# Packing the time-step columns into four partition groups, moving the parameter loads to SyncE's queue, and starting two output blocks behind the scan

## The chip, the cores and the metric

The kernel runs on one core of one Trainium2 chip. The metric is the device time in microseconds of one execution (us). TensorE (PE) does the matmuls, and its weight loads are listed as PEld; VectorE (DVE), ScalarE (ACT) and GpSimd (POOL) do the elementwise work; SyncE (SP) and the other engines issue transfers (a DMA issue of ScalarE's own queue is listed as ACTq, of SyncE's as SPq).

## The reference, cut to what matters

The whole is a decoder step with two layers over 512 prompt tokens and 64 sample tokens (8 sequences of 8), 576 tokens in all, model width 1024. Layer 0 is a Mamba-2 mixer (2048 inner channels, 32 heads) and an MLP, layer 1 a sparse attention and an MLP. The change touches layer 0's mixer alone:

```
zxbcdt = h @ in_w                                  # 1024 -> z 2048, x/B/C 3072, dt 32
z, xbc, dt = split(zxbcdt)
xbc, new_conv = causal_conv(xbc, conv_state, conv_w, conv_b)      # 4 taps, then silu
dt = softplus(dt + dt_bias)                        # one number for each token and head
A = -exp(a_log)                                    # the scan uses x*dt and a = dt*A
y, h_last = ssd_scan(xs * dt, dt * A, B, C, h0)    # chunks of 128 tokens
y = (y + xs * d_skip) * silu(z)
y = y * rsqrt(mean over each of 4 groups of y*y + eps) * norm_w
mix = y @ out_w                                    # 2048 -> 1024
h = layer_norm(alpha * h + mix)
```

## The kernel before

**Layout.** Activations lie feature by partition: `xT` holds the input as 8 chunks of 128 features by 576 tokens. Every dense product is done in fp32r with both operands split into a rounded part (hi) and the rest (lo), and three products (hi·hi, hi·lo, lo·hi) are summed. A weight slot is 128 x 1024 numbers (512 KB). There are two slots: SyncE loads one into `ring` (L596 for the first two, L603 for the others), ScalarE writes its hi part (`split_hi`, L943, semaphore `w_hi`), GpSimd its lo part (`split_lo`, L697, semaphore `w_split`), then the ring slot may be loaded again. A block is one slot times all tokens: `dense_block` (L1299) runs over 8 chunks k, three products, two halves of 288 tokens, so 48 matmuls, into one of two pairs of PSUM banks; `w_used` tells that a block is done, `blk_evac` that its banks have been read.

**Start.** ScalarE first issues the loads of `dtw` (the 32 time-step columns of the weights, L930), of x in four parts of 2 chunks (L932, 576 KB each) and of 12 parameter tiles (L934, 0.72 MB together: bias and log A in `dtb`, identity, triangles, masks, conv weights, norms). Then it splits slot 0, rounds x into `xs[:, 0]` (L983, chunk by chunk), and splits slot 1. VectorE makes the lo part of x (L1822, semaphore `x_split`). TensorE first does the time-step product with `dtw` in plain fp32: for each k a matmul of 512 prompt tokens into bank `bX` and one of 64 sample tokens into `bM`, both into partitions 0 to 31 (L1360, L1361). In the trace each fp32 matmul is two instructions. Then come blocks 0 to 9 of group 0.

**Time steps.** ScalarE waits for all parameters (`s_par`) and for the product, adds the bias, takes the absolute value and exp (L989 to L993) on 32 x 576. VectorE computes softplus with a polynomial (L1825 to L1837: 17 operations on 32 x 576, one of them a reciprocal, most of them waiting for the one before) and only then turns to the causal conv of blocks 0 to 4 (L1851 for 512 tokens and L1853 for 64, three of each for a block). After block 4 TensorE transposes the steps and a = dt·A to token by head (L1371, L1372, 10 transposes), and VectorE copies them out (`dt_tok`, `a_tok`), which lets `segment_rows` and the decays start.

**ScalarE's order in blocks 0 to 9** is written out by hand:

```
for blk in range(GB):
    evac(blk)
    split_hi(blk + 2)
    if blk:
        conv_silu(blk - 1)
```

`evac` copies the block's banks to `raw` (L1011 to L1014) and writes the first conv tap (L1021 to L1024). `conv_silu(blk - 1)` (L1040) waits until VectorE has finished that block's conv. Whatever stands behind it in this order waits too.

**Scan.** 20 tiles (4 groups g, 5 token tiles c) follow; between the parts of a tile TensorE does "filler" blocks: the next group's input blocks, or in the last group the first half of the output projection. The last group's y is squared and summed over partitions (`squares_sum`, L1491), VectorE and ScalarE form the root and its reciprocal (L1884, L1059, L1889), scale y (L1891), round it (L1064) and make its lo part (L1974, semaphore `y_split`). Then comes `last_projection(0, ...)`: the second half of the output projection, 8 blocks that sum over y's tiles 8 to 15. Tiles 8 to 11 are of group 2 and are ready earlier, 12 to 15 are of the last group. Its block 0 waits chunk by chunk for `y_split`, the means of the layer norm (L1336) follow block 1. `finish_his` and `finish_los` split the later slots.

Of the kernel before, what the change touches and what calls it, by code (L numbers as in the profile page):

```python
# [28 lines left out]
ACT = mybir.ActivationFunctionType  # L29
AX = mybir.AxisListType  # L30

P = 128
D = 1024
KC = D // P
NP_TOK = 512
NB, NS = 8, 8
ND = NB * NS
T = NP_TOK + ND
HT = T // 2
# [6 lines left out]
MH, MP, MN, MG = 32, 64, 128, 4  # L46
# [23 lines left out]
NSLOT = 2  # L70
NT = 5
# [14 lines left out]
def build(nc, a):  # L86

    with ExitStack() as ctx:
# [8 lines left out]
        dense = ctx.enter_context(nc.psum_tensor("dense", [P, 4, 512], F32))  # L97
# [3 lines left out]
        bX, bM = bXM[:, 0, :], bXM[:, 1, :]  # L101
# [4 lines left out]
        split = sb("split", [P, NSLOT, 2, SLOT], F32R)  # L106
        ident = sb("ident", [P, P])
        triu = sb("triu", [P, 2, P])
# [19 lines left out]
        def carve(*shape, parts=P):  # L128

            first = at[0]  # L130
            at[0] += int(np.prod(shape))
            assert at[0] <= ARENA, at[0]
            tiles.append(nc.alloc_sbuf_tensor_at(f"tile{len(tiles)}", [parts, *shape], F32,
                                                 offset=arena_at + 4 * first, align_bytes=4))
            return tiles[-1][tuple(slice(0, n) for n in (parts, *shape))]
# [6 lines left out]
        xT = carve(KC, T)  # L142
# [15 lines left out]
        y_lo = split_tile("y_lo", at[0] - DI // P * T, DI // P, T)  # L158
        y_hi = xs.rearrange("p s k t -> p (s k) t")
        at[0] = xs_end  # L160
        dtT = carve(T, parts=MH)
        dw = [carve(T, parts=MH) for _ in range(4)]
        aT = carve(T, parts=MH)
        at[0] = xs_end + (XB + DI // P) * T
        cst = carve(NXB, NB, 3)
        lastp = carve(NXB, 3)
# [3 lines left out]
        nw = carve(DI // P)  # L170
        dsk = carve(DI // P)
        dtw = carve(KC, MH)
        dtb = carve(2, parts=MH)
        smask = carve(NB, parts=ND)
        dt_tok = carve(NT, MH)
        a_tok = carve(NT, MH)
# [110 lines left out]
        S_M1, S_M2, s0 = [], [], SL_IN + SL_OUT  # L287
        B_OUT = (SL_IN, SL_IN + KC)
        B_M1, B_M2, b0 = [], [], SL_IN + 2 * KC
        for layer in range(2):  # L290
# [6 lines left out]
            if layer == 0:  # L297
# [3 lines left out]
                s0, b0 = S_O + SL_O, B_O + KC  # L301
        assert s0 == N_SLOTS

        PARAM_TILES = ((dtw, "dtw"), (dtb, "dtb"), (ident[:, :], "ident"), (triu[:, :, :], "triu"),
                       (low[:, :, :], "low"), (smask, "smask"), (cst, "cst"), (cw, "cw"), (cb, "cb"),
                       (nw, "nw"), (dsk, "dsk"), (lng[:, :, :], "lng"), (lnb[:, :, :], "lnb"))
        N_PARAMS = len(PARAM_TILES)
# [8 lines left out]
        s_par = sem("params_loaded")  # L316
# [3 lines left out]
        w_split = sem("slots_split")  # L320
        w_used = sem("slots_used")
# [8 lines left out]
        blk_evac = sem("block_evacuated")  # L330
# [8 lines left out]
        dt_tok_ready = sem("dt_by_token")  # L339
# [118 lines left out]
        def link(eng, who, ins):  # L458

            s = dve_step if who == "dve" else act_step  # L460
            ins.then_inc(s, 1)
            steps[who] += 1
            eng.wait_ge(s, steps[who])

        def width(c):
            return P if c < 4 else ND

        def tok(c):
            return slice(c * P, c * P + width(c))
# [124 lines left out]
        def _(sp):  # L594
# [3 lines left out]
            def stream(first, last):  # L598
                with sp.Fori(first // NSLOT, last // NSLOT) as i:
                    for j in range(NSLOT):  # L600

                        sp.wait_ge(w_split, i * NSLOT + (j + 1 - NSLOT))
                        sp.dma_start(ring[:, j, :], a["w"][i * NSLOT + j, :, :]).then_inc(w_ready[j], 16)  # L603

            stream(NSLOT, S_OUT[0] + 2 * NSLOT)

            sp.wait_ge(xbc_ready, NXB)
# [320 lines left out]
        def _(act):  # L928
            for dst, name in PARAM_TILES[:1]:
                act.dma_start(dst, a[name]).then_inc(s_dtw, 16)  # L930
            for q in range(4):
                act.dma_start(xT[:, 2 * q:2 * q + 2, :], a["x"][:, 2 * q:2 * q + 2, :]).then_inc(s_x[q], 16)  # L932
            for dst, name in PARAM_TILES[1:]:
                act.dma_start(dst, a[name]).then_inc(s_par, 16)  # L934

            def split_hi(s, i=None):

# [48 lines left out]

            act.wait_ge(s_par, 16 * (N_PARAMS - 1))
            act.wait_ge(dt_done, 1)
            act.activation(dtT[:, 0:NP_TOK], bX[0:MH, :], ACT.Identity, bias=dtb[:, 0:1])  # L989
            link(act, "act", act.activation(dtT[:, NP_TOK:T], bM[0:MH, 0:ND], ACT.Identity, bias=dtb[:, 0:1]))  # L990
            link(act, "act", act.activation(dw[0], dtT, ACT.Abs))
            act.activation(dw[1], dw[0], ACT.Exp, scale=-1.0)
            act.activation(dtb[:, 1:2], dtb[:, 1:2], ACT.Exp).then_inc(dt_abs, 1)  # L993
# [72 lines left out]
            for g, c, n in TILES:  # L1066
                L = width(c)
# [94 lines left out]
            for own in range(2):  # L1162
                for m in range(4):
                    kv, gp = divmod(m, 2)
                    for half in range(2):
                        ps = slice(half * HD, half * HD + HD)
                        src = kvT[ps, m, 0:NP_TOK].rearrange("p (c j h) -> p j h c", c=NCMP, h=2)
# [106 lines left out]
        def _(pe):  # L1274
# [43 lines left out]
            def by_token(out, part, v):  # L1318
# [3 lines left out]
                                   start=True, stop=True)  # L1322
                return mm

            def last_projection(k, hi, lo, ready=None):

                b0, s0, nsl, _ = ENDS[k]
                for j in range(2):
                    dense_block(b0 + j, s0 + j * nsl, nsl, hi, lo, ready=ready if j == 0 else None)

                pe.wait_ge(blk_evac, b0 + 1)
                if k == 0:

                    pe.wait_ge(st_ready, MG * (4 + NB))
                for cols in (slice(0, 512), slice(512, T)):
                    mm = pe.matmul(flat_x[:, cols], onesd[:, :], xT[:, 0, cols], start=True, stop=True)  # L1336
                mm.then_inc(ln_tok, 1)
                with pe.Fori(1, KC // 2 - 1) as i:
                    for j in range(2):
                        dense_block(b0 + j, s0 + j * nsl, nsl, hi, lo, i, 2 * nsl)  # L1340
                dense_block(b0 + KC - 2, s0 + (KC - 2) * nsl, nsl, hi, lo)

                def squares(kk):
                    if kk == nsl * KC - 2:
                        pe.wait_ge(ln_added, 6 * (k + 1))
                        by_token(s2, 0, SQS[k])

                dense_block(b0 + KC - 1, s0 + (KC - 1) * nsl, nsl, hi, lo, after=squares)
# [8 lines left out]
            for k in range(KC):  # L1357
                pe.wait_ge(s_x[k // 2], 16)
                ends = dict(start=k == 0, stop=k == KC - 1)
                pe.matmul(bX[0:MH, :], dtw[:, k, :], xT[:, k, 0:NP_TOK], **ends)  # L1360
                mm = pe.matmul(bM[0:MH, 0:ND], dtw[:, k, :], xT[:, k, NP_TOK:T], **ends)  # L1361
            mm.then_inc(dt_done, 1)
            in_block(0, (x_split, 0))
            for blk in range(1, 5):
# [1 line left out]
            pe.wait_ge(s_par, 16 * (N_PARAMS - 1))  # L1366

            pe.wait_ge(dt_ready, 1)
            for c in range(NT):
                L = width(c)  # L1370
                pe.transpose(bX[0:L, c * 64:c * 64 + MH], dtT[:, tok(c)], ident[0:MH, 0:MH])  # L1371
                mm = pe.transpose(bX[0:L, c * 64 + MH:c * 64 + 64], aT[:, tok(c)], ident[0:MH, 0:MH])  # L1372
            mm.then_inc(dt_tr, 1)
            in_block(5)
            in_block(6)
# [2 lines left out]
            for c in range(NT):  # L1378
                L = width(c)
                pe.matmul(bS[0:L, 0, c * MH:(c + 1) * MH], low[0:L, c // 4, 0:L], a_tok[0:L, c, :],  # L1380
                          start=True, stop=True)
            for c in range(4):
                pe.matmul(bS[:, 0, (NT + c) * MH:(NT + c + 1) * MH], ones[:, :], a_tok[:, c, :],
                          start=True, stop=True)
            pe.matmul(bS[:, 1, 0:NB * MH], ones[0:ND, :], am.rearrange("p b h -> p (b h)"),
                      start=True, stop=True).then_inc(dec_sum, 1)
# [429 lines left out]
        def _(dve):  # L1816
# [51 lines left out]
                conv(blk)  # L1868

            dve.wait_ge(dt_tr, 1)  # L1870
            tr = bX[:, 0:NT * 64].rearrange("p (c k h) -> p c k h", c=NT, k=2)
            dve.tensor_copy(dt_tok[:, 0:4, :], tr[:, 0:4, 0, :])
            dve.tensor_copy(dt_tok[0:ND, 4, :], tr[0:ND, 4, 0, :])
            dve.tensor_copy(a_tok[:, 0:4, :], tr[:, 0:4, 1, :])
            dve.tensor_copy(a_tok[0:ND, 4, :], tr[0:ND, 4, 1, :]).then_inc(dt_tok_ready, 1)
            for blk in range(5, GB):
                conv(blk)

# [570 lines left out]
```

## Time and profile before

| what | value |
|---|---|
| time before, median of 3 runs | 2104.06 us (2100.3 to 2104.97) |
| profiled execution: its time | 2098.91 us |
| profiled execution: span | 2097.2 us |
| TensorE busy | 1942.2 us (93%) |
| VectorE, ScalarE, GpSimd busy | 816.4, 705.8, 961.4 us |
| granted clock of TensorE, mean | 0.952 |

The span runs from the first instruction to the last; times in views are counted from its start. The granted clock is the share of TensorE's 2.4 GHz that it was given (1.00, or 0.50 for 1.2 GHz; a value between them is a stretch with both). An idle time in square brackets is that of the instruction's own engine before it, with the releaser behind the arrow.

### The profile page before, as it was taken

The page shows a single profiled execution, that of the slowest core. Times are in us where ns is not written, and L with a number is a line of the kernel's source. Part 1 is how long each engine was busy: PE and PEld are TensorE (multiplying, and loading weights), DVE is VectorE, ACT ScalarE, POOL GpSimd, SP SyncE. Part 2 cuts the span into 40 slices and gives each one's busy share as a digit, 9 for nine tenths or more (in the row PEclk, how much of TensorE's full clock was granted, in tenths as well). Part 3 has the DMA queues.
Part 4 walks back from the last instruction along what each step waited for, and adds up shares of the span by engine and source line. Part 5 has one row for each costly group of instructions (what it writes and reads, how often), then busy time and mean ns, then how long its engine had stood idle before and what let it go on. Part 6 is the DMA issues. An engine that isn't in the chain of part 4 may idle for free. (4 is left out here: it accounts for less than half of the span.)

```text
span 2097.2 us, 36461 instructions
## 1 busy us (share of the span) xinstructions
PE 1942.2 (93%) x14668; PEld 1773.5 (85%) x14668; DVE 816.4 (39%) x1567; ACT 705.8 (34%) x1292; POOL 961.4 (46%) x685
## 2 busy tenths in 40 slices
PE   7998899988888998999999999899978899999996
PEld 5987887867778998999998998755548899999996
DVE  7364573746455220022233112378655521012134
ACT  4453553634134221122223131266533322122222
POOL 2445454444447643356444342454403565346552
PEclk9998999989998999999999999799999899999998
DMA  4211312113131226332221333420161122222221
GB/s 163 80 51 41 121 51 111 51 70 127 41 117 62 80 72 172 90 121 82 81 79 51 127 136 109 173 78 1 41 222 41 51 81 90 81 81 80 82 82 64
DMA packets 61077, 185.12 MB, mean 88 GB/s; under 512 B 15519, under 2 KB 20287, under 8 KB 59425
## 3 DMA queue, kind: packets, MB, share of 16 engines
q1 hardware_dynamic: 48720, 130.18, 18.9%
q0 software_dynamic: 9952, 50.08, 6.7%
q10 hardware_dynamic: 2288, 3.23, 0.4%
q8 instruction: 83, 1.36, 0.3%
q14 instruction: 34, 0.27, 0.0%
HBM read 167.05 MB, written 27.35 MB: 93 GB/s over the span
## 5 line engine op out<-in xcount | busy, mean ns | idle before, releaser
L1299 PE MATMUL dense<-xs,split 128*128 128x288 f32 x6848 | 978.3, 301 | 28.2 <-POOL xs L805 8.5
L1299 PEld LDWEIGHTS dense<-xs,split 128*128 128x128 f32 x6848 | 942.0, 192 | 63.2 <-issue 43.5
L697 POOL TENSOR_TENSOR split<-ring,split 128x1024 fp32r<-128x1024 f32 x212 | 533.7, 2518 | 815.7 <-ACT split L943 793.7
L943 ACT ACTIVATE split<-ring 128x1024 fp32r<-128x1024 f32 x212 | 223.9, 1056 | 798.2 <-PE dense L1299 775.4
L1299 PE MATMUL dense<-hid,split 128*128 128x288 f32 x3072 | 415.8, 298 | 5.8 <-POOL split L697 5.8
L1299 PEld LDWEIGHTS dense<-hid,split 128*128 128x128 f32 x3072 | 414.3, 191 | 6.0 <-POOL split L697 6.0
L1863 DVE SCALAR_TENSOR_TENSOR tile<-tile,dense 128x576 f32<-128x576 f32 (+1 forms) x56 | 42.2, 754 | 422.0 <-PE dense L1299 422.0
L2032 DVE TENSOR_SCALAR sq<-dense 128x576 f32<-128x576 f32 x64 | 48.5, 757 | 310.5 <-PE dense L1299 310.5
L914 POOL TENSOR_SCALAR tile<-tile,tile,tile 128x128 f32<-128x128 f32 (+3 forms) x128 | 77.8, 622 | 80.8 <-DVE tile L2195 80.8
L1851 DVE SCALAR_TENSOR_TENSOR tile<-tile,tile,tile 128x512 f32<-128x512 f32 x72 | 87.5, 1215 | 41.2 <-ACT tile L1024 39.4
L816 POOL TENSOR_TENSOR hid<-sq,hid 128x576 f32 x64 | 77.3, 1208 | 0.0
L1201 ACT ACTIVATE tile<-tile,tile 128x128 f32<-128x128 f32 (+3 forms) x128 | 70.4, 553 | 18.1 <-DVE tile L2180 17.9
L1632 PE MATMUL dense<-tile,tile 128*128 128x128 f32 x576 | 66.4, 274 | 0.8 <-issue 0.8
L1632 PEld LDWEIGHTS dense<-tile,tile 128*128 128x128 f32 x576 | 64.9, 188 | 1.9 <-issue 1.2
L1998 DVE SCALAR_TENSOR_TENSOR tile<-tile,tile 128x576 f32<-128x576 f32 x24 | 61.8, 2575 | 0.0
L1148 ACT ACTIVATE hid<-sq 128x576 f32 x64 | 43.9, 686 | 44.3 <-DVE sq L2035 44.3
L1299 PE MATMUL dense<-y_lo,split 128*128 128x288 f32 x256 | 56.6, 303 | 0.0
L1672 PE MATMUL dense<-tile,tile 64*128 64x128 f32 (+3 forms) x128 | 47.8, 491 | 6.1 <-DVE tile L2172 4.6
L1715 PE MATMUL dense<-tile,tile 128*64 128x256 f32 x384 | 52.0, 392 | 0.0
L1672 PE MATMUL bS<-tile,tile 64*128 64x128 f32 (+3 forms) x128 | 49.1, 496 | 0.4 <-DVE tile L2135 0.4
L2035 DVE TENSOR_TENSOR sq<-sq 128x576 f32<-128x576 f32 x64 | 48.6, 759 | 2.2
L1028 ACT ACTIVATE tile<-dense 128x576 f32<-128x576 f32 x16 | 10.4, 652 | 108.3 <-PE dense L1299 108.3
(316 smaller groups left out, 2118.2 us busy)
## 6 DMA issues: line engine op xcount, KB each, us to landing
ring<-in_w SPq DMA_DIRECT2D x212, 512.0 KB, 3.3
tile<-in_state POOLq DMA_DIRECT2D x4, 2048.0 KB, 9.2
o_sssm<-tile POOLq DMA_DIRECT2D x4, 2048.0 KB, 7.5
tile<-in_cmp POOLq DMA_DIRECT2D x32, 256.0 KB, 3.2
tile<-in_win POOLq DMA_DIRECT2D x8, 1024.0 KB, 5.9
tile<-in_sel SPq DMA_DIRECT2D x32, 256.0 KB, 5.2
o_kv<-tile POOLq DMA_DIRECT2D x1, 3456.0 KB, 12.2
bskew<-bscr SPq DMA_DIRECT2D x1, 3072.0 KB, 22.3
```

The source lines that it names most:

```text
L697: pool.tensor_tensor(split[:, j, 1, :], ring[:, j, :], split[:, j, 0, :].bitcast(F32), ALU.subtract).then_inc(w_split, 1)
L816: pool.tensor_tensor(hid[:, 1, m, :], sq[:, j, :], hid[:, 0, m, :].bitcast(F32), ALU.subtract).then_inc(hid_ready, 1)
L914: last = pool.tensor_scalar(pb(u, r)[:, 0:n], pb(u, r)[:, 0:n], wt[:, u % 2, r:r + 1], gate, ALU.mult, ALU.mult)
L943: act.activation(split[:, j, 0, :], ring[:, j, :], ACT.Copy).then_inc(w_hi, 1)
L1201: last = act.activation(pb(u, r)[:, 0:n], pb(u, r)[:, 0:n], ACT.Exp, bias=nmx[:, u % 4, r:r + 1], accum_out=sm[:, u % 4, r:r + 1])
L1299: mm = pe.matmul(dense[:, 2 * par + h_, 0:HT], split[:, j, w, cols], v[:, kk, h_ * HT:(h_ + 1) * HT], start=kk == 0 and t == 0, stop=kk == ...
L1632: mm = pe.matmul(dense[:, 2 * (s_ % 2) + kv, r * P:(r + 1) * P], cw1[:, kv, r, j, :], rows, start=j == 0, stop=j == 7)
L1672: pe.matmul(SB[k][:, 0:(qt + 1) * P], qT[half_of(h_), gp * GR + r, tok(qt)], kvT[half_of(h_), 4 * (br + 1) + gp, 0:(qt + 1) * P], start=Tr ...
L1715: mm = pe.matmul(OBANK[half_of(g), rr * 2 * P:(rr + 1) * 2 * P], v, PT[t % 4][:, h_ * 2 * P:(h_ + 1) * 2 * P], start=br == 0 and kt == 0, ...
L1851: dve.scalar_tensor_tensor(o[:, 0:NP_TOK], r[:, k:k + NP_TOK], cw[:, x, k:k + 1], o[:, 0:NP_TOK], ALU.mult, ALU.add)
L1998: link(dve, "dve", dve.scalar_tensor_tensor(xT[:, m, :], xT[:, m, :], alpha, CEN[k], ALU.mult, ALU.subtract))
L2035: dve.tensor_tensor(h, h, h, ALU.mult).then_inc(hid_sq, 1)
```

## The change

1. The time-step product gives four prompt tiles of 128 tokens in partitions 32q to 32q+31 (q = 0 to 3) of `bX`, 128 columns wide, and the 64 sample tokens four times over in `bM`. So `dtT`, `dw` and `aT` become 128 partitions x 192 columns; `dtb` is loaded four times. The softplus works on 128 x 192, and 4 transposes (two of 128 x 128) take the place of 10.
2. SyncE issues the parameter loads (now 15) behind the first two slots and ahead of the rest of the weights; ScalarE issues only `dtw` and x.
3. In the last projection of layer 0, blocks 0 and 1 are done as chunks 0 to 3 of both, then chunks 4 to 7 of both.

```diff
-        dtT = carve(T, parts=MH)
-        dw = [carve(T, parts=MH) for _ in range(4)]
-        aT = carve(T, parts=MH)
+        dtT = carve(P + ND)
+        dw = [carve(P + ND) for _ in range(4)]
+        aT = carve(P + ND)
...
-        dtb = carve(2, parts=MH)
+        dtb = carve(2)
...
-        PARAM_TILES = ((dtw, "dtw"), (dtb, "dtb"), (ident[:, :], "ident"), (triu[:, :, :], "triu"),
+        PARAM_TILES = ((dtw, "dtw"), *((dtb[q * MH:(q + 1) * MH], "dtb") for q in range(4)), (ident[:, :], "ident"), (triu[:, :, :], "triu"),
...
+            for dst, name in PARAM_TILES[1:]:
+                sp.dma_start(dst, a[name]).then_inc(s_par, 16)
             stream(NSLOT, S_OUT[0] + 2 * NSLOT)
...
-            for dst, name in PARAM_TILES[1:]:
-                act.dma_start(dst, a[name]).then_inc(s_par, 16)
...
-            act.activation(dtT[:, 0:NP_TOK], bX[0:MH, :], ACT.Identity, bias=dtb[:, 0:1])
-            link(act, "act", act.activation(dtT[:, NP_TOK:T], bM[0:MH, 0:ND], ACT.Identity, bias=dtb[:, 0:1]))
+            act.activation(dtT[:, 0:P], bX[:, 0:P], ACT.Identity, bias=dtb[:, 0:1])
+            link(act, "act", act.activation(dtT[:, P:P + ND], bM[:, 0:ND], ACT.Identity, bias=dtb[:, 0:1]))
...
+            def early_chunks(b0, s0, hi, lo, ready):
+                for ks in (range(0, 4), range(4, KC)):
+                    for j in range(2):
+                        if ks[0] == 0:
+                            pe.wait_ge(blk_evac, b0 + j - 1)
+                            pe.wait_ge(w_split, s0 + j + 1)
+                        for k in ks:
+                            if j == 0:
+                                pe.wait_ge(ready[0], ready[1] + k + 1)
+                            for t, (w, v) in enumerate(((0, hi), (0, lo), (1, hi))):
+                                for h_ in range(2):
+                                    mm = pe.matmul(dense[:, 2 * ((b0 + j) % 2) + h_, 0:HT],
+                                                   split[:, (s0 + j) % NSLOT, w, k * P:(k + 1) * P],
+                                                   v[:, k, h_ * HT:(h_ + 1) * HT],
+                                                   start=k == 0 and t == 0, stop=k == KC - 1 and t == 2)
+                        if ks[0]:
+                            mm.then_inc(w_used, 1)
...
+                if k == 0:
+                    early_chunks(b0, s0, hi, lo, ready)
                 for j in range(2):
-                    dense_block(b0 + j, s0 + j * nsl, nsl, hi, lo, ready=ready if j == 0 else None)
+                    if k:
+                        dense_block(b0 + j, s0 + j * nsl, nsl, hi, lo, ready=ready if j == 0 else None)
...
-                pe.matmul(bX[0:MH, :], dtw[:, k, :], xT[:, k, 0:NP_TOK], **ends)
-                mm = pe.matmul(bM[0:MH, 0:ND], dtw[:, k, :], xT[:, k, NP_TOK:T], **ends)
+                for bank, n in ((bX, P), (bM, ND)):
+                    for q in range(4):
+                        mm = pe.matmul(bank[q * MH:(q + 1) * MH, 0:n], dtw[:, k, :],
+                                       xT[:, k, q * P:q * P + n] if n == P else xT[:, k, NP_TOK:T], **ends)
...
-            for c in range(NT):
-                L = width(c)
-                pe.transpose(bX[0:L, c * 64:c * 64 + MH], dtT[:, tok(c)], ident[0:MH, 0:MH])
-                mm = pe.transpose(bX[0:L, c * 64 + MH:c * 64 + 64], aT[:, tok(c)], ident[0:MH, 0:MH])
+            for i, src in enumerate((dtT, aT)):
+                o = i * NT * MH
+                pe.transpose(bX[:, o:o + P], src[:, 0:P], ident[:, :])
+                mm = pe.transpose(bX[0:ND, o + P:o + NT * MH], src[0:MH, P:P + ND], ident[0:MH, 0:MH])
...
-            tr = bX[:, 0:NT * 64].rearrange("p (c k h) -> p c k h", c=NT, k=2)
-            dve.tensor_copy(dt_tok[:, 0:4, :], tr[:, 0:4, 0, :])
+            tr = bX[:, 0:NT * 64].rearrange("p (k c h) -> p k c h", k=2, c=NT)
+            dve.tensor_copy(dt_tok[:, 0:4, :], tr[:, 0, 0:4, :])
```

## Rows read from the trace of the kernel before

**Rows 1.** Waits of TensorE, 0 to 60 us (total us, times, longest).

```profile
PE bXM L1360 <- DMA tile<-in_x: 7.7, 1, 7.7
PE dense L1299 <- POOL split L697: 6.9, 1, 6.9
```

**Rows 2.** Timeline, 0 to 60 us (start us, length us, engine, line).

```profile
9.78 1.28 ACT L943 ACT_TABLE_LOAD   x1 [9.78 <-issue]
...
12.04 4.68 ACT L983 ACTIVATE xs<-tile 128x576 fp32r<-128x576 f32 x8
...
12.74 9.34 DVE L1822 TENSOR_TENSOR xs<-tile,xs 128x576 fp32r<-128x576 f32 x8 [12.74 <-ACT xs L983]
...
18.28 26.21 PE L1299 MATMUL dense<-xs,split 128*128 128x288 f32 x192
...
22.48 3.74 DVE L1826 RECIPROCAL tile<-tile 32x576 f32<-32x576 f32 x1
...
27.03 0.75 DVE L1828 TENSOR_TENSOR tile<-tile 32x576 f32<-32x576 f32 x1
...
28.30 9.60 DVE L1831 SCALAR_TENSOR_TENSOR tile<-tile,tile 32x576 f32<-32x576 f32 x7
28.36 2.95 POOL L697 TENSOR_TENSOR split<-ring,split 128x1024 fp32r<-128x1024 f32 x1 [5.86 <-ACT split L943]
...
41.13 0.91 DVE L1866 MEMSET tile<- 64x1024 f32 x1 [0.27 <-issue]
...
42.73 0.28 DVE L1853 SCALAR_TENSOR_TENSOR tile<-tile,tile,tile 128x64 f32<-128x64 f32 x1
...
45.01 0.69 ACT L1040 ACTIVATE tile<-tile 128x576 f32<-128x576 f32 x1 [9.10 <-DVE tile L1853]
...
48.88 2.34 POOL L697 TENSOR_TENSOR split<-ring,split 128x1024 fp32r<-128x1024 f32 x1 [11.59 <-ACT split L943]
...
51.37 7.94 PE L1299 MATMUL dense<-xs,split 128*128 128x288 f32 x48 [6.88 <-POOL split L697]
```

**Rows 3.** DMA issues by line: first and last start, then time to landing.

```profile
L596 SPq DMA_DIRECT2D ring<-in_w x2: 387/404/422, 0.9 to 1.3; - x2
DMA to landing us min/median/max: 4.0/4.9/5.9
L932 ACTq DMA_DIRECT2D tile<-in_x x4: 451/495/723, 1.3 to 3.1; - x4
DMA to landing us min/median/max: 6.2/7.5/8.6
L934 ACTq DMA_DIRECT2D lnb<-in_lnb x1: 504/504/504, 9.2 to 9.2; - x1
DMA to landing us min/median/max: 5.9/7.3/8.2
```

**Rows 4.** The time-step product by line (ns min/median/max, first and last start).

```profile
L1360 PE MATMUL bXM<-tile,tile x16: 592/592/1061, 7.7 to 17.6; 128*32 128x512 f32 x16
```

**Rows 5.** Timeline of TensorE, fp32 matmuls onto 32 partitions each.

```profile
556.05 1.92 PE L1432 MATMUL bXM<-tile,tile 128*32 128x512 f32 x16
...
1533.88 1.70 PE L1782 MATMUL dense<-tile,tile 128*32 128x64 f32 x88 [1.10 <-ACT tile L1252]
```

**Rows 6.** Timeline behind the scan, 587 to 610 us.

```profile
596.00 2.76 DVE L1974 TENSOR_TENSOR y_lo<-tile,xs 128x576 fp32r<-128x576 f32 x4
...
596.81 0.85 PE L1299 MATMUL dense<-xs,split 128*128 128x288 f32 x2 [5.96 <-DVE y_lo L1974]
...
608.07 1.19 PE L1336 MATMUL bXM<-tile,onesd 128*128 128x512 f32 x4
```

**Rows 7.** Idle TensorE in the scan (timeline).

```profile
136.12 1.09 PE L1406 MATMUL bXM<-ident,tile 128*128 128x128 f32 x4 [2.22 <-DVE tile L1957]
```

**Rows 8.** Windows: length, busy of PE, PEld, DVE, ACT, POOL, clock, DMA share, GB/s.

```profile
136.10:139.00 2.90, 2.88 (x14) 2.90 (x15) 1.09 (x3) 2.88 (x4) 1.76 (x1) 0.50 0.02 6
...
596.80:600.00 3.20, 3.19 (x13) 3.19 (x14) 1.96 (x3) 0.09 (x1) 0.00 (x0) 0.50 0.00 0
```

More of the change, by code:

```diff
@@ L1870, in _ @@
             dve.wait_ge(dt_tr, 1)
-            tr = bX[:, 0:NT * 64].rearrange("p (c k h) -> p c k h", c=NT, k=2)
-            dve.tensor_copy(dt_tok[:, 0:4, :], tr[:, 0:4, 0, :])
-            dve.tensor_copy(dt_tok[0:ND, 4, :], tr[0:ND, 4, 0, :])
-            dve.tensor_copy(a_tok[:, 0:4, :], tr[:, 0:4, 1, :])
-            dve.tensor_copy(a_tok[0:ND, 4, :], tr[0:ND, 4, 1, :]).then_inc(dt_tok_ready, 1)
+            tr = bX[:, 0:NT * 64].rearrange("p (k c h) -> p k c h", k=2, c=NT)
+            dve.tensor_copy(dt_tok[:, 0:4, :], tr[:, 0, 0:4, :])
+            dve.tensor_copy(dt_tok[0:ND, 4, :], tr[0:ND, 0, 4, :])
+            dve.tensor_copy(a_tok[:, 0:4, :], tr[:, 1, 0:4, :])
+            dve.tensor_copy(a_tok[0:ND, 4, :], tr[0:ND, 1, 4, :]).then_inc(dt_tok_ready, 1)
             for blk in range(5, GB):
```

## The prediction

> **What bounds the kernel now.** I read the page first: TensorE is busy for 93% of the span, so a change counts only where TensorE stands idle or works longer than it must. The list of TensorE's waits in the first 60 us [rows 1] has two entries: 7.7 us until the first part of x has landed, and 6.9 us at block 4, which has no split weights yet. The timeline of that stretch [rows 2] tells why. Blocks 0 to 3 run without a gap from 18.28 to 44.49 us, 6.55 us each. The next one starts at 51.37, released by GpSimd's lo part, which itself sat idle for 11.59 us for ScalarE's hi part. ScalarE had been idle for 9.10 us in the silu of block 0's conv, released by VectorE's last conv operation at 45.0. VectorE could not begin a conv before 42: it was at the softplus polynomial from 22 to 41 us. So the wait of 6.9 us is VectorE's softplus, handed on through ScalarE's order and GpSimd. The second place is behind the scan [rows 6]: TensorE has done chunks 0 to 3 of the output block and is idle for 5.96 us until VectorE's first `y_split` of the last group. Both waits are longer than they look, because TensorE comes back at its lower rate: block 4 takes 7.94 us in place of 6.55 [rows 2], and from 596.8 to 600 the granted clock is 0.50, which is 1.2 GHz [rows 8].
>
> **Part 1a, the softplus on 128 x 192.** A VectorE operation with two tensors takes 0.75 us at 576 columns and 0.28 at 64 [rows 2], so 0.28 + 128/512 x 0.47 = 0.40 at 192 and 0.43 with the step to the next. The number of partitions should not matter: the 128-partition conv row lies on the line of the 32-partition one only if it doesn't, and I have no other row. Eleven operations of this kind make 4.7 us, the reciprocal a third of 3.74 = 1.25, five with one tensor at most 0.3 each = 1.5. Sum 7.4. In the kernel before, the 17 take 19 us, of which some 4 us are two operations held while GpSimd runs a lo part: the seven of the polynomial take 9.60 where 7 x 0.78 = 5.5 would do, with a GpSimd operation of 2.95 us inside [rows 2]. One such hold may fall into the shorter chain: 7.4 to 9.8, I take 8.6. ScalarE's four operations ahead of it get shorter too, which I count at nothing.
>
> **Part 1b, the time-step product.** The number of columns is 4 x 128 for the prompt as before, but 4 x 64 in place of 64 for the samples, and there are 16 instructions for each k in place of 4. What decides is whether products onto different groups of 32 partitions overlap. They do in the scan [rows 5]: 16 fp32 instructions of 512 columns take 1.92 us where one alone lasts 0.43 behind another (592 ns with its fixed part, [rows 4]), so nearly four at a time. 88 of 64 columns take 1.70 us, 0.019 each. Then a k costs 8 x 128/512 x 0.12 = 0.24 plus 8 x 0.019 = 0.15, together 0.39 at the full rate and 0.7 to 0.8 at half of it. Before, a k took 1.9 us at first (1061 ns an instruction) and 1.0 later (592 ns), in all 10.6 us from 7.7 to 18.28 [rows 2, 4]. Eight k are now at most 6 us, so the arrival of x bounds this stage. If they don't overlap, a k is 1.28 at the full rate: (512 + 256)/(512 + 64) times 0.97. The Trainium skill, TensorEngine Tiling (Array Packing), section "Instruction Overhead", speaks against thin tiles: each matmul has about 60 cycles of overhead, and one should not tile a dimension that is small already. By it, and calling this an estimate, the 128 instructions are not under 3.2 us at 2.4 GHz (6.4 at 1.2), against 3.1 (about 6) by the rows; the sum would be the same by either.
>
> **Part 2, the parameters on SyncE.** ScalarE issued 12 loads at about 0.5 us each up to 9.75, and only then could load its table and split slot 0 (9.78, ready at 12.04), although slot 0 had landed at 0.9 + 4.0 = 4.9 us [rows 2, 3]. Now it is ready for slot 0 at 4.9, so slot 0 is split by 8.5, and x's chunks are rounded as they land (0.6 us each, VectorE's lo part 0.76 each without a hold). On SyncE 15 issues take 1.75 to 9.4 us. Nothing behind them is late: the next slot was issued at about 14.7, behind the lo part of slot 0, and now can go at 9.4. But transfers share the 16 DMA engines. Before, the parameters stood behind x in one queue, and x's parts landed at 7.5 to 11.7 us. How two queues share is to be seen at slot 1: it landed at 1.3 + 5.9 = 7.2, together with x's first part at 7.5, so about half each. Between those two x rows 3 x 0.59 MB pass in 4.2 us, 0.42 MB/us. With equal shares, 0.72 MB of parameters and 0.5 MB of the next slot get ahead of x: 1.22/0.42 = 2.9 us, x complete at 14.6. Unshared, it is 11.7. The Trainium skill, DMA: Bandwidth & Descriptors, section "Queues, rings and completion order", says that each DMA engine takes its queue rows in turn, packet by packet. The two landings agree; by it x lands at 14.6, without it the sum below would be 2.9 us more of a gain. I take 14.6.
>
> Last two k of the product after 14.6: 1.4 us at half rate, so block 0 begins at 16.0. Its chunks are never late: the last x chunk is rounded at 15.8 and its lo part is there by 17. The work ahead of it now has gaps, so the clock may still be at 1.2 GHz for the first 3 us; I charge 0.7 (between 0 and 1.5). Block 0 ends at 16.0 + 6.55 + 0.7 = 23.2, against 18.28 + 6.55 = 24.8. **Gain 1.6** (1.0 to 2.4; 3.9 to 5.3 with x unshared).
>
> Then the chain behind it: ScalarE splits slot 1 (to 16.9; its lo part by 19.4, before block 1), waits for the parameters (the last issued at 9.0 lands 5.9 to 8.2 us later [rows 3], so by about 16) and hands over at 18.3. VectorE is done at 27, with the memset of 0.9 at 28, and needs 3.0 us for a conv (5.4 with a hold): block 0's is done by 31 to 33.5. ScalarE wants it for the silu once block 1's evacuation and slot 3's hi part are through, at about 23.2 + 6.55 + 3.3 = 33. So the stall of block 4 goes. What is late next is the pair of splits: before, the lo part for block 2 ended 31.31 - 24.83 = 6.5 us after block 0, just one block's time [rows 2]; as before it costs nothing or tenths. **Gain 6.9, and 1.4** for block 4 at the full rate.
>
> Fewer transposes (4 for 10, next to four of 128 columns in 1.09 us at half rate [rows 7]): **0.2**. The scan's tiles wait for this in no other way; all behind moves as a whole.
>
> **Part 3, behind the scan.** Weights of both blocks are split and the second's banks are free before the scan's end, so TensorE has chunks 0 to 3 of block 1 to fill the 5.96 us: 24 matmuls, 3.3 us. After 596.8 there are 8 chunks left where 12 were done, 596.8 to 608.07 = 11.3 us, of which 1.6 is the lower clock. If the clock falls in the 2.7 us of idleness that stay, then 6.55 + 1.6 = 8.1 are left, a gain of 3.2; if it holds, 4.7. An idle stretch of 2.22 us in the scan was followed by 0.50 [rows 7, 8], so I take 3.4. Slot 2's split follows block 0's end at about 601.5 by 1.1 + 2.4 us = 605, the means run until then (604.9 to 606). **Gain 3.4.**
>
> **Sum.** 1.6 + 6.9 + 1.4 + 0.2 + 3.4 = 13.5. The profiled execution, 2098.9 us (span 2097.2 and 1.7 around it), becomes 2085.4. It was 5.2 us below the median of the runs, 2104.06; set against that median the forecast is 2090.6.
>
> **Rivals.** (a) x is not delayed, because the parameter transfers, some with few bytes for a partition, get less than half: gain 13.5 + 2.9 = 16.4 and a warm clock some more, 2087. Against: the landings of slot 1 and x. Chance 0.10. (b) The narrow matmuls do not overlap, because here each pair onto one group comes in a row and every instruction changes x. Two k at half rate (5.1) and six at 1.28 (7.7) end at 20.7; block 0 ends at 27.3, 2.5 us later than before: gain 9.4, 2094.7. Against: the order of the row at L1432 is the same pair by pair. Chance 0.10. (c) The stall at block 4 stays in part, with two holds of VectorE and late tables: it takes 5 us more of lateness than I count to cost the first microsecond. Half of it would leave 9.5, 2094.6. Chance 0.05. (d) Given back in the scan: TensorE's idle stretches of about 2 us there sit at the point where the clock falls or holds. Each that tips costs 1.5; seven would leave 3, 2101, no change. Chance 0.04. (e) Slower: ScalarE waits for all parameters before it may evacuate block 0. Every us that they land after about 22 delays all that follows; at 22 + 14 = 36 the gain is gone, at 40 it is 4.2 us slower, 2108. Small loads would have to take 31 us from issue, against 5.9 to 8.2 in the row. Chance 0.05 with anything of its kind. My forecast has 0.66.
>
> **How the numbers follow.** 0.2% of 2104 is 4.2 us, about what a measurement of this kernel can tell from no change. Faster: forecast, (a), (b), (c), 0.91; I say 0.90. Same 0.05, slower 0.05. The range: the largest gain is x unshared with the full clock, 5.3 + 8.5 + 4.7 = 18.5, 2085.5, and 1.5 of scatter (the three runs span 4.7): 2084. The upper end takes in (b) and (c) at 2094.7 and 2 us of scatter and of clock: 2097.
>
> **What would show it.** ScalarE's first table load near 4 us and the first hi part near 5 to 6. The last x landing at 14.6 (11.7 by (a)). The eight k at 0.8 us or less each, block 0 beginning near 16. VectorE's 17 operations in 7.4 to 9.8 us. No wait of TensorE for GpSimd at block 4, the transposes near 49.4 in place of 59.2. Behind the scan 48 matmuls ahead of the wait, which falls to 2.7 us, and the means (L1336) 8 us behind its end in place of 11.3. Wrong it would be if x landed last at 17 or more, or the scan's idle time grew by more than 3 us.

## The result and the profile after

| | time, median (lowest to highest) | profiled execution: time, span |
|---|---|---|
| before, 6 runs | 2101.32 us (2097.8 to 2104.97) | 2098.91, 2097.2 us |
| changed, 6 runs | 2086.28 us (2084.36 to 2091.26) | 2088.06, 2086.4 us |

The ratio is 0.9931, with a 95% interval of 0.9913 to 0.9948: 14.5 us faster (10.9 to 18.3). Two later comparisons of the same pair of kernels gave 0.9917 (0.9894 to 0.9940) and 0.9926 (0.9905 to 0.9947). The forecast was 13.5 us, or 2090.6 us against the median of the first three runs. An interval this wide cannot tell 13.5 from 16.

The page of the changed kernel has nearly the same busy times as before; what went is idle time:

```profile
PE 1938.6 (93%) x14758; PEld 1776.7 (85%) x14758; DVE 806.6 (39%) x1567; ACT 705.7 (34%) x1292; POOL 959.2 (46%) x685
```

TensorE's waits in the first 60 us, changed kernel. The wait for GpSimd at block 4 [rows 1] is not there any more:

```profile
PE bXM L1386 <- DMA tile<-in_x: 9.5, 3, 8.0
```

The timeline of the same stretch, against [rows 2]:

```profile
3.75 1.28 ACT L944 ACT_TABLE_LOAD   x1 [3.75 <-issue]
...
7.97 1.51 PE L1386 MATMUL bXM<-tile,tile 128*32 128x128 f32 x32 [7.97 <-DMA tile<-in_x]
...
10.66 3.09 PE L1386 MATMUL bXM<-tile,tile 128*32 128x128 f32 x64 [1.18 <-DMA tile<-in_x]
...
14.08 1.51 PE L1386 MATMUL bXM<-tile,tile 128*32 128x128 f32 x32 [0.33 <-DMA tile<-in_x]
...
15.52 24.71 PE L1300 MATMUL dense<-xs,split 128*128 128x288 f32 x181
...
18.11 0.73 DVE L1851 TENSOR_SCALAR tile<-tile 128x192 f32<-128x192 f32 x1 [1.92 <-ACT tile L994]
...
20.26 0.36 DVE L1853 TENSOR_TENSOR tile<-tile,tile 128x192 f32<-128x192 f32 x1
...
21.34 2.73 DVE L1857 SCALAR_TENSOR_TENSOR tile<-tile,tile 128x192 f32<-128x192 f32 x7
...
25.95 0.91 DVE L1892 MEMSET tile<- 64x1024 f32 x1 [0.27 <-issue]
...
33.48 0.69 ACT L1041 ACTIVATE tile<-tile 128x576 f32<-128x576 f32 x1
...
47.94 0.27 PE L1397 MATMUL bXM<-ident,tile 128*128 128x128 f32 x1
```

The reader is to see four things. ScalarE's first work starts at 3.75 us in place of 9.78. The product for two k (32 instructions) takes 1.51 us, and TensorE waits for each part of x. The softplus goes from 18.11 to 25.7 us, 7.6 us in place of 19, and the seven operations of the polynomial take 2.73 us in place of 9.60. The silu of block 0 (33.48) comes right behind its table load without an idle time, where ScalarE had waited 9.10 us, so the dense blocks run through to the transposes, which begin at 47.94.

The landing of x (changed kernel): the last is 3.1 + 11.0 = 14.1 us, against 11.7 before [rows 3]. The first line is the issues, the second the time to landing:

```profile
L935 ACTq DMA_DIRECT2D tile<-in_x x4: 453/552/738, 1.3 to 3.1; - x4
...
DMA to landing us min/median/max: 6.5/9.3/11.0
```

Behind the scan, the timeline against [rows 6]. The idle time in front of chunk 4 is 2.72 us in place of 5.96, and the means come 6.5 us behind the end of that idle time in place of 11.3:

```profile
593.77 0.53 PE L1339 MATMUL dense<-xs,split 128*128 128x288 f32 x2 [2.72 <-DVE y_lo L2000]
...
600.28 1.19 PE L1360 MATMUL bXM<-tile,onesd 128*128 128x512 f32 x4
```

So far this is 11.2 us won at the start and 4.8 behind the scan, 16.0 us. The two profiled spans differ by 10.8. Where the rest is, windows over three stages show: from block 5 to the last squares of the scan, from there to the means, and the rest. The columns are length, busy time of PE, PEld, DVE, ACT, POOL, granted clock, DMA share, GB/s. First before, then changed:

```profile
59.92:587.27 527.35, 476.08 (x3378) 420.81 (x3377) 281.50 (x366) 234.50 (x456) 256.83 (x171) 0.93 0.21 76
587.27:608.07 20.80, 14.85 (x98) 14.56 (x97) 10.95 (x11) 5.06 (x8) 2.38 (x1) 0.84 0.35 126
608.07:2097.20 1489.13, 1406.07 (x10916) 1300.84 (x10914) 479.95 (x1140) 439.71 (x771) 684.90 (x495) 0.96 0.27 89
```

```profile
48.69:584.23 535.54, 482.88 (x3377) 426.33 (x3377) 283.31 (x368) 234.72 (x456) 256.25 (x171) 0.92 0.21 75
584.23:600.28 16.05, 13.33 (x99) 13.04 (x98) 10.95 (x11) 5.06 (x8) 1.80 (x1) 1.00 0.38 137
600.28:2086.40 1486.12, 1403.27 (x10916) 1299.66 (x10914) 480.02 (x1140) 439.76 (x771) 684.84 (x496) 0.96 0.28 90
```

The rest behind the means is 3.0 us shorter, which is scatter: it took 1490.5 us in the second profile of the kernel before and 1492.5 and 1488.8 in the other two of the changed one. The scan's stage is 8.2 us longer in the changed kernel with the same instructions; 6.8 of it is TensorE's busy time at a lower granted clock (0.92 for 0.93). Whether the change does that or the clock scatters was open, and the repeats below were made for it.

### The profile page after: what moved, and what is told of

Read it like the earlier page. It is cut to its first block and busy times, and to the rows that moved or that the text cites. A ratio compares the mean times of both kernels' runs of the same rounds, so it can differ in the third digit from the quotient of the medians.

```text
span 2086.4 us, 36644 instructions
## 1 busy us (share of the span) xinstructions
PE 1938.6 (93%) x14758; PEld 1776.7 (85%) x14758; DVE 806.6 (39%) x1567; ACT 705.7 (34%) x1292; POOL 959.2 (46%) x685
## 3 DMA queue, kind: packets, MB, share of 16 engines
q1 hardware_dynamic: 50432, 130.92, 19.3%
## 5 line engine op out<-in xcount | busy, mean ns | idle before, releaser
L1300 PE MATMUL dense<-xs,split 128*128 128x288 f32 x6784 | 967.3, 301 | 14.5 <-POOL xs L808 7.7
L1877 DVE SCALAR_TENSOR_TENSOR tile<-tile,tile,tile 128x512 f32<-128x512 f32 x72 | 94.0, 1305 | 42.4 <-ACT tile L1025 40.7
L1698 PE MATMUL bS<-tile,tile 64*128 64x128 f32 (+3 forms) x128 | 49.4, 497 | 0.4 <-DVE tile L2161 0.4
L1300 PE MATMUL dense<-y_lo,split 128*128 128x288 f32 x224 | 49.4, 303 | 0.0
## 6 DMA issues: line engine op xcount, KB each, us to landing
o_kv<-tile POOLq DMA_DIRECT2D x1, 3456.0 KB, 12.2
```

The costliest lines, as they stand in the source:

```text
L1300: mm = pe.matmul(dense[:, 2 * par + h_, 0:HT], split[:, j, w, cols], v[:, kk, h_ * HT:(h_ + 1) * HT], start=kk == 0 and t == 0, stop=kk == ...
L1698: pe.matmul(SB[k][:, 0:(qt + 1) * P], qT[half_of(h_), gp * GR + r, tok(qt)], kvT[half_of(h_), 4 * (br + 1) + gp, 0:(qt + 1) * P], start=Tr ...
L1877: dve.scalar_tensor_tensor(o[:, 0:NP_TOK], r[:, k:k + NP_TOK], cw[:, x, k:k + 1], o[:, 0:NP_TOK], ALU.mult, ALU.add)
```

## The experiments

**Each part by itself, and all again.** The four ran on one chip, beside 26 runs of the kernel before (median 2100.72 us). For `e1_pack_only` the parameter loads go back and the early chunks are left out:

```diff
-            for dst, name in PARAM_TILES[1:]:
-                sp.dma_start(dst, a[name]).then_inc(s_par, 16)
...
             for q in range(4):
                 act.dma_start(xT[:, 2 * q:2 * q + 2, :], ...)
+            for dst, name in PARAM_TILES[1:]:
+                act.dma_start(dst, a[name]).then_inc(s_par, 16)
...
-                if k == 0:
-                    early_chunks(b0, s0, hi, lo, ready)
```

> Part 1 alone: time steps on 128 x 192, ScalarE still issues the parameters, no early chunks. Theory (softplus is the cause of the stall at block 4): the stall is gone here already. ScalarE begins at 9.8 us as before, so x's lo parts are ready late and block 0 ends near 22.9 in place of 24.8. Gain 1.9 + 6.9 + 1.4 + 0.2 = 10.4 us, ratio 0.9950. Rival (the stall is ScalarE's late start): the stall stays in part, the gain is 5 us or less, ratio 0.9975 or more.

Measured: 0.9952 (0.9935 to 0.9968), 10.1 us. The stall of block 4 is nearly gone with part 1 alone, although ScalarE starts later than before, so the late start was not its cause; that the softplus was, `e5` below shows. The ratio is what I expected, but the first 60 us are not, so that agreement is in part luck. Waits of TensorE, and the timeline of ScalarE and TensorE, in this run:

```profile
PE bXM L1363 <- DMA tile<-in_x: 8.1, 2, 7.9
PE dense L1300 <- DVE xs L1825: 4.1, 1, 4.1
PE dense L1300 <- POOL split L698: 0.5, 1, 0.5
```

```profile
11.36 1.28 ACT L944 ACT_TABLE_LOAD   x1 [11.36 <-issue]
...
38.98 0.69 ACT L1041 ACTIVATE tile<-tile 128x576 f32<-128x576 f32 x1 [2.29 <-DVE tile L1856]
```

ScalarE now issues 15 parameter loads, not 12, because the bias is loaded four times, and starts its first work at 11.36 us, 1.6 us later than in [rows 2]. I had counted with 9.8. TensorE, done with its short product at 12.9, waits 4.1 us for the first lo chunk of x; VectorE is late as well, the silu waits 2.29 us for the conv, and 0.5 us of the stall is left. After the 4.1 us of idleness TensorE begins block 0 at its lower clock, 0.50 up to 20 us:

```profile
16.90:20.00 3.10, 3.09 (x13) 3.10 (x14) 3.10 (x5) 3.07 (x7) 0.68 (x1) 0.50 0.50 169
```

Block 5 starts at 52.68 us, 7.2 us earlier than before (8.3 against the second profile of the kernel before, below).

`e2_params_only` is the kernel before with the loads moved:

```diff
+            for dst, name in PARAM_TILES[1:]:
+                sp.dma_start(dst, a[name]).then_inc(s_par, 16)
             stream(NSLOT, S_OUT[0] + 2 * NSLOT)
...
-            for dst, name in PARAM_TILES[1:]:
-                act.dma_start(dst, a[name]).then_inc(s_par, 16)
```

> Part 2 alone: SyncE issues the parameters, everything else as before. Theory: TensorE's wide product still bounds block 0's begin at about 18.3 (x is complete later, at 14), VectorE's softplus starts 1 us earlier, so the stall at block 4 shrinks by 1 us: gain 1 us, ratio 0.9995 (0.9985 to 1.0005). Rival (ScalarE's late start matters): gain 4 us or more, ratio 0.998 or less.

Measured: 1.0000 (0.9983 to 1.0017). ScalarE is early here too, but TensorE's wide product ends at 18.6 and the softplus is as long as ever. TensorE's waits:

```profile
PE bXM L1360 <- DMA tile<-in_x: 8.1, 1, 8.1
PE dense L1299 <- POOL split L699: 6.2, 1, 6.2
```

x's last part lands at 2.9 + 10.2 = 13.1 us here, against 11.7 to 12.2 in the four profiles with the parameters behind it:

```profile
L934 ACTq DMA_DIRECT2D tile<-in_x x4: 453/531/800, 1.3 to 2.9; - x4
DMA to landing us min/median/max: 6.6/8.4/10.2
```

`e3_early_only` is the kernel before with `early_chunks` and its call.

> Part 3 alone: chunks 0 to 3 of both blocks first. Theory: 24 matmuls fill 3.2 us of the wait behind the scan, and the clock holds as it did in the changed kernel: gain 3.2 to 4.8 us, ratio 0.9978 to 0.9985. Rival (what is gained is lost to the later split of slot 2): gain under 1.5 us, ratio above 0.9993.

Measured: 0.9989 (0.9974 to 1.0004), 2.3 us, an interval that holds no change too. The stage itself is clear: in its windows it takes 17.59 us in place of 20.80, 3.2 less, at a granted clock of 0.90.

```profile
586.05:603.64 17.59, 14.83 (x99) 14.55 (x98) 10.95 (x11) 5.05 (x8) 1.81 (x1) 0.90 0.34 125
```

What is gained is not lost again to the later split of slot 2: the stage behind the means took 1489.3 us on the average of the seven profiles with part 3 and 1489.6 in the five without it (1486.1 to 1493.8 in all).

> The changed kernel once more, beside its parts on one chip. If the parts add, its gain is that of the three single parts within 2 us: 13.5 to 15.5 us, ratio 0.9926 to 0.9936. The stage from the transposes of the time steps to the end of the scan's squares, 535.5 us in the first profile of it against 527.4 before, should scatter with TensorE's granted clock: I expect 525 to 537 in this profile and in those of the parts, though none of them changes anything in it. Rival: the change itself lengthens that stage, then it is above 533 in every kernel with part 1 and below 530 in the others.

Measured: 0.9917 (0.9894 to 0.9940), 17.4 us. The single parts sum to 10.1 + 0.0 + 2.3 = 12.4 us. The intervals would allow equality; the start of block 5, which is the same in the profiles of one kernel within 1.1 us, does not: part 1 brings 7.2 (to 8.3), part 2 alone 0.4 (to 1.4), both together 11.2 to 13.0.

**Parts 1 and 2 without part 3.** The edit is `e1`'s without its first two pieces, so only the early chunks are out.

> Parts 1 and 2 without the early chunks. Theory: part 2 adds to part 1 only what block 0 ends earlier, 0.5 to 1 us: gain 10.5 to 11.5 us over the kernel before, 3.2 to 4.8 us less than the whole change. Rival (part 3 costs as much as it brings): as fast as the whole change.

Measured: 0.9947 (0.9932 to 0.9962), 11.1 us. Block 5 starts at 48.47 us, 4.2 us before that of part 1 alone, so part 2 is worth much more beside part 1 than the 0.5 to 1 us that I gave it. Of the 4.2, block 0 beginning earlier (15.28 for 16.91) makes 1.6, the rest of the stall 0.5, and the lower clock behind the idle time 2.1 (34.7 us of blocks 0 to 4 in `e1`, 32.6 here). In the times of the two kernels it does not show; their intervals overlap, and this profile's scan took 535.5 us.

**Lateness put back.** `e5_late_softplus` is the changed kernel with VectorE kept busy:

```diff
             link(dve, "dve", dve.tensor_scalar(dw[2], dw[1], 2.0, None, ALU.add))
+            for _ in range(6):
+                link(dve, "dve", dve.reciprocal(dw[3], dw[2]))
```

> The changed kernel with six needless reciprocals of 128 x 192 in the softplus, 6 x 1.38 = 8.3 us of VectorE time (their result is overwritten). Theory (block 4's weights hang on VectorE's first conv): in the profile of the changed kernel the conv of block 0 is done at 31.0 us, ScalarE wants it at 32.2 and has 1.2 us of idleness behind it, then 0.4 is left at block 4, so 2.8 us are free and the other 5.5 show as a wait of TensorE for GpSimd at block 4 of 4 to 5.5 us, and 1.4 more for the clock: 4 to 7 us slower than the changed kernel. By the slack of 5 us that my prediction counted: 3.3 us. Rival (the softplus is not the cause): no wait at block 4 and no slower than 1 us.

Measured: 0.9962 (0.9949 to 0.9975), 8.0 us faster than before, so 6.5 to 9.4 us slower than the changed kernel by its three ratios, where I expected 4 to 7. The wait at block 4 is back in the list of TensorE's waits, and the first 5.5 us of block 4 run at the low rate; timeline below it:

```profile
PE dense L1300 <- POOL split L700: 5.7, 1, 5.7
```

```profile
15.04 25.86 PE L1300 MATMUL dense<-xs,split 128*128 128x288 f32 x192
46.56 9.15 PE L1300 MATMUL dense<-xs,split 128*128 128x288 f32 x48 [5.66 <-POOL split L700]
```

Block 4 took 9.15 us in place of 6.55, another 2.6 for the clock where I had counted 1.4, and block 5 begins 8.1 us later than the average of the changed kernel's profiles (56.31 against 48.2). This is the chain that the prediction named, shown by putting it back.

How much lateness was free is not the difference of 8.3 and 5.66, because more than the added work moved. First the changed kernel (conv of block 0, its last operation, GpSimd's lo part for block 4), then this run (the seven operations of the polynomial, the silu of block 0):

```profile
26.88 1.96 DVE L1877 SCALAR_TENSOR_TENSOR tile<-tile,tile,tile 128x512 f32<-128x512 f32 x1
...
30.72 0.28 DVE L1879 SCALAR_TENSOR_TENSOR tile<-tile,tile,tile 128x64 f32<-128x64 f32 x1
...
38.64 2.38 POOL L700 TENSOR_TENSOR split<-ring,split 128x1024 fp32r<-128x1024 f32 x1 [4.01 <-ACT split L944]
```

```profile
29.57 4.88 DVE L1859 SCALAR_TENSOR_TENSOR tile<-tile,tile 128x192 f32<-128x192 f32 x7
...
40.20 0.69 ACT L1041 ACTIVATE tile<-tile 128x576 f32<-128x576 f32 x1 [7.52 <-DVE tile L1881]
```

The polynomial was held for 2.2 us here (4.88 for 2.73) and the conv for 1.2 less (0.75 for 1.96), so the conv was done 9.2 us later, at 40.16 for 31.00. TensorE had also finished block 3 some 0.8 us earlier (40.9 for 41.7). Of 10.0 us of lateness against TensorE 5.66 became a wait, so 4.3 us were free. The changed kernel's own rows give nearly the same: 2.5 us from the conv's end (31.00) to the silu (33.48), 1.2 of idleness of ScalarE before the next evacuation, and 0.7 from the lo part's end (41.02) to block 4. My count of 2.8 for this run left out that the table load does not wait for the conv, and that a hold can move.

**x over two queues.** `e6_x_on_two_queues` is the changed kernel with:

```diff
+            for q in (1, 3):
+                sp.dma_start(xT[:, 2 * q:2 * q + 2, :], a["x"][:, 2 * q:2 * q + 2, :]).then_inc(s_x[q], 16)
             for dst, name in PARAM_TILES[1:]:
                 sp.dma_start(dst, a[name]).then_inc(s_par, 16)
...
-            for q in range(4):
+            for q in (0, 2):
                 act.dma_start(xT[:, 2 * q:2 * q + 2, :], a["x"][:, 2 * q:2 * q + 2, :]).then_inc(s_x[q], 16)
```

> The changed kernel, but SyncE issues the second and fourth part of x, ahead of the parameters, and ScalarE only the first and third. Theory (x is late because the parameters share the engines with it): x is complete near 11.7 us as in the kernel before, in place of 14.0, block 0 begins near 13.2 in place of 15.5, and it is 2 to 3 us faster than the changed kernel. Rival (something else sets the begin of block 0 or of block 4, for one the parameters, which land at 16 or later): under 1 us faster.

Measured: 0.9908 (0.9893 to 0.9922), 19.3 us. SyncE's two parts land by 2.3 + 9.5 = 11.8 us. Its timeline:

```profile
L607 SPq DMA_DIRECT2D tile<-in_x x2: 432/504/576, 1.8 to 2.3; - x2
...
DMA to landing us min/median/max: 8.2/8.9/9.5
```

```profile
10.04 3.81 PE L1388 MATMUL bXM<-tile,tile 128*32 128x128 f32 x96 [0.47 <-DMA tile<-in_x]
13.78 32.71 PE L1302 MATMUL dense<-xs,split 128*128 128x288 f32 x240
```

x was late in the changed kernel because of the parameters: without them ahead of its parts, it lands as in the kernel before. (This run also gives x two queues, but in the kernel before one was enough for 11.7.) Block 0 begins at 13.78 us in place of 15.52 (15.04 to 15.52 over the profiles of that path), and the transposes at 46.33 in place of 47.94 (47.19 in the second profile). That is 0.9 to 1.6 us, less than the 2 to 3 expected. The time is 1.9 to 4.8 us below the changed kernel's by its three ratios, which were taken elsewhere, and all these intervals overlap.

`e9_queues_and_memset` also moves VectorE's memset of `Bm` from behind the softplus to the head of its program.

> x over both queues, and VectorE's memset of 0.9 us moved from behind the softplus to the beginning, where VectorE has nothing to do. In the profile of e6 ScalarE waited 1.9 us at the silu for the conv of block 0, but TensorE had no wait at block 4. Theory: that wait shrinks to 1 us and nothing else moves, so it is as fast as e6 within 0.5 us, and 2 to 3 us faster than the changed kernel beside it: ratio to the kernel before 0.9915 to 0.9925. Rival (the clock's scatter in the scan decides): the two differ in either direction by up to 4 us with no difference in the first 50 us.

> The changed kernel for a third time, beside e9 on one chip, since its ratio came out as 0.9931 and 0.9917. By its parts 0.993: 14.5 us faster than before. Its stage from the transposes to the end of the scan's squares was 535.5 and 527.0 us in two profiles: 525 to 536 again. Rival (the first profile was the rule): above 533.

Measured side by side: 0.9921 (0.9899 to 0.9943) for `e9`, 0.9926 (0.9905 to 0.9947) for the changed kernel, medians 2082.58 and 2084.25 us. The transposes begin at 45.22 and at 47.25 us. So 2 us are won in the first 50, and the medians differ by 1.7, but the intervals do not part the two. A version that measurably beats the changed kernel was not found.

**The kernel before once more.**

> The kernel before, unchanged: ratio 1, within 0.1%. Its profile gives a second look at the stage from the transposes to the end of the scan's squares, 527.4 us in the first. Clock scatter: 525 to 537. Rival (that stage is longer only where the time steps are packed): 527 again within 1.

Measured: 0.9996 (0.9986 to 1.0006). The stage took 525.4 us, 2.0 less than in the first profile of the same kernel, and TensorE's wait at block 4 was 7.94 us where the first had 6.88:

```profile
60.95:586.33 525.38, 474.25 (x3380) 420.88 (x3377) 283.63 (x366) 234.16 (x456) 257.78 (x171) 0.94 0.21 76
```

The windows of the scan's stage in the other two profiles of the changed kernel, `e4` and then `e10`, with the stage behind it:

```profile
47.94:574.93 526.99, 474.37 (x3378) 421.14 (x3377) 283.43 (x368) 234.62 (x456) 256.67 (x171) 0.94 0.21 76
574.93:592.51 17.58, 14.82 (x98) 14.54 (x97) 10.95 (x11) 5.05 (x8) 1.81 (x1) 0.90 0.35 125
```

```profile
48.00:575.34 527.34, 475.90 (x3378) 422.51 (x3377) 284.25 (x368) 234.48 (x456) 257.81 (x171) 0.93 0.21 76
575.34:592.88 17.54, 14.82 (x98) 14.53 (x97) 10.95 (x11) 5.05 (x8) 1.79 (x1) 0.90 0.35 125
```

The same stage, of the same instructions, over all profiles: before 527.4 and 525.4; part 2 alone 531.5; part 3 alone 524.9; part 1 alone 526.0; parts 1 and 2 535.5; changed 535.5, 527.0, 527.3; late softplus 529.1; x on two queues 528.2; with the memset 533.9. The changed kernel has 535.5 and 527.0 with no edit between them, and with part 1 there are five values under 530. Between the first two profiles of the changed kernel 8.5 of the 8.55 us are TensorE's busy time (482.88 and 474.37). So the 8 us that the first profile lost in the scan are scatter of the clock, not a fixed cost of the change. That the change makes the long scan more frequent is not excluded: it is above 533 in three of eight profiles with part 1 and in none of four without it.

## Why the prediction was right

**The cause of the stall** held: softplus, conv, silu, hi part, lo part, block 4. Packing the softplus removed it, and putting 8.3 us back restored it. The softplus took 7.6 us where I took 8.6 out of 7.4 to 9.8: no operation of the polynomial was held in the changed kernel (some were in `e1` and `e5`). An operation of 192 columns took 0.36 us (0.40 estimated). That partitions cost nothing shows at 576 columns: 0.75 us on 32 partitions [rows 2] and 0.76 on 128, in x's lo part:

```profile
L1848 DVE TENSOR_TENSOR xs<-tile,xs x8: 750/756/760, 8.6 to 15.4; 128x576 fp32r<-128x576 f32 x8
```

**The slack behind it** had about the right size: the prediction let the first microsecond of wait come 5 us after its own count for the conv (31 to 33.5); the conv came at 31.0, and 4.3 us more were free before the wait began. What a wait there costs it had too low: the clock took 1.4 us in the first profile of the kernel before, about 2.2 in the second (block 4 in 8.79 us) and 2.6 in `e5`.

**The narrow product** overlaps, rival (b) is out: two k in 1.51 us are 0.76 for one, against 0.7 to 0.8 at half rate. In `e1`, where the last two k ran at 0.87 us for both, one is 0.44 (0.39 estimated at the full rate). The prediction's floor of 6.4 us for the 128 instructions at 1.2 GHz does not hold: in `e7` they took four times 1.51, 6.0 us, at the slow rate.

**x** landed last at 14.1 us, near the 14.6 of the sum, but not by its working, so the nearness is in part luck. The sum let 1.22 MB pass ahead of x at 0.42 MB/us, by equal shares of the two queues; the landings that it read them from were not quite equal (1.05 MB from SyncE's queue and 0.72 from ScalarE's by 7.5 us). In fact the next slot was issued only at 11.18 us, and between x's first part and its last (7.9 to 14.1 us) the windows add up to some 2.0 MB, of which 1.77 are x's: I estimate 0.6 us for the parameters' bytes. The greater part, about 1.4 us, is a stretch in which the engines moved less than half of the 0.42. Here are the changed kernel and then part 2 alone, whose loads differ in `dtb` only, one in place of four:

```profile
8.00:9.00 1.00, 1.00 (x24) 1.00 (x28) 0.43 (x1) 1.00 (x2) 0.52 (x1) 1.00 0.80 189
9.00:10.00 1.00, 0.47 (x15) 0.23 (x7) 1.00 (x2) 0.11 (x1) 0.00 (x0) 1.00 0.71 185
```

```profile
8.00:10.00 2.00, 1.93 (x5) 0.61 (x6) 1.33 (x2) 1.64 (x3) 0.70 (x1) 1.00 1.03 409
```

So part 2 by itself delays x by 0.9 to 1.4 us (`e2`), and another 0.7 to 1.0 (13.8 to 14.1 for 13.1) comes with the three further loads of `dtb`, small as they are; `e6`, with the parameters behind x's parts, shows neither. The Trainium skill's rule that each DMA engine takes its queue rows in turn (DMA: Bandwidth & Descriptors, "Queues, rings and completion order") agrees with the trace in that SyncE's first parameters landed at 7.8 us, while x was still arriving on the other queue; no run shows equal shares of the bytes. Block 0 began at 15.52 (16.0) and ended at 22.5 (23.2), a gain of 2.4 for the 1.6 of the sum. The transposes came at 47.94 in place of 49.4: 11.3 us won up to there, 9.8 forecast.

**Behind the scan** the gain is 3.2 us or 4.8 as the clock falls or holds in the 2.7 us of idleness. It held in the first profile (16.05 us for the stage, clock 1.00), in `e6` and in `e9`, and fell in `e3`, `e4`, `e5` and `e10` (17.5 to 17.6, clock 0.90). The 3.4 of the sum is near the gain with the clock fallen, which came in four profiles of seven.

**Given back in the scan** (rival d) was seen in the first profile, 8.2 us where the rival had 10.5, and is no fixed property of the change. The clock scatters in the kernel before too: in the 11 runs of `e8` the time goes with the mean granted clock, from 2097.5 us at 0.952 to 2105.7 at 0.949, and the lowest and highest run of that kernel on one chip lie 7 to 14 us apart. That single stretches of idleness tip it is shown behind the scan and argued for the scan itself.

**What I did not see** is that parts 1 and 2 need each other. Part 2 alone is worth nothing, since the wide product and the long softplus hide it. Part 1 alone brings less than I thought, since its three more loads of the bias delay ScalarE by 1.6 us and since TensorE, done with its short product, then waits 4.1 us for x's lo part and comes back at the lower clock. The sum was made for both together and so stood.

**The sum.** By the averages over all profiles of the two kernels, 12.2 us are won up to block 5 (60.4 to 48.2) and 3.2 to 4.8 behind the scan, 15.4 to 17.0 in all, where the sum had 10.1 and 3.4. The three comparisons gave 14.5, 17.4 and 15.5 us, 15.8 on the average. So the sum was some 2 us low, mostly at block 0 and in the stall with its clock, and that the first comparison came within 1 us of it is luck.

## What to carry to other kernels

A wait of TensorE for its weights can have its cause three engines away; follow the list of idle times back until an engine was busy, and ask what it was busy with. Elementwise work on 32 of 128 partitions is worth folding into four groups where it lies in an ordered queue, and the matmuls that feed it can write the four groups in parallel. When one part of a change makes the work ahead of a point short, look at what else arrives there, as here the order in which ScalarE issues loads: measured alone, such a part looks worth nothing. Three more tiny loads are not free either where the first work waits for a transfer beside them.

## What the runs showed of the hardware

The same idle stretch of TensorE, 2.7 us behind the scan, left the granted clock at 1.00 in some executions and brought it down in others of the same kernel (1.5 us of difference). The scan took 527.0 and 535.5 us in two profiles of one kernel for the same instructions, and nearly all of the difference was TensorE's busy time at a lower granted clock (0.94 and 0.92). After 4.05 us of idleness in `e1` the granted clock was 0.50 for 3 us, and block 0 paid for it. In the first 13 us the clock column reads 1.00 although matmuls took 1.7 times their later time (1.51 us for 32 instructions against 0.87 in `e1`): there the durations tell the rate, not the column. In the five profiles with parts 1 and 2 and x on one queue the DMA engines moved 171 to 247 GB/s between 8 and 10 us, against 409 in `e2`, which loads `dtb` once and not four times. The last of the 15 parameter issues on SyncE took 1.43 us where the others took 0.42 to 0.63, and the next slot's load went out at 11.18 us where the prediction had 9.4; nothing waited for it.
